# Down projection weights loaded as neighbouring rows, the activation written in even and odd order

## The reference

```
top_val, top_idx = lax.top_k(logits, TOP_K)            # 4 of 32
gates = jax.nn.softmax(top_val, axis=-1)
hgu = lax.ragged_dot(xs, w_gate_up, group_sizes) + b_gate_up[e_sorted]   # 1024 -> 2048
x_glu = jnp.minimum(hgu[..., ::2], 7.0)
x_lin = jnp.clip(hgu[..., 1::2], -7.0, 7.0)
act = x_glu * jax.nn.sigmoid(1.702 * x_glu) * (x_lin + 1.0)              # 1024 per token
out = lax.ragged_dot(act, w_down, group_sizes) + b_down[e_sorted]        # 1024 -> 1024
out = out * gates.reshape(-1)[order][:, None]
```

## Time and profile before

| | |
|---|---|
| three runs, median | 1988.65 us (1988.04 to 1990.12) |
| the profiled execution, its own time | 1986.01 us |
| its span, first to last instruction | 1984.3 us |
| mean granted clock of TensorE | 0.984 |
| TensorE / VectorE / ScalarE busy | 1932.5 / 1703.8 / 1372.4 us |
| one item of the loop, from one bias matmul to the same of the next item | 35.48 us |

### The profile page before, as it was taken

How to read it: one execution, slowest core, us unless ns; L and a number is a source line. 1 busy time by engine, 2 the same in 40 slices (tenths; PEclk the granted TensorE clock), 3 DMA queues, 4 the chain that set the end, 5 groups by cost and what they waited for, 6 DMA issues and landing times.

```text
span 1984.3 us, 29677 instructions
## 1 busy us (share of the span) xinstructions
PE 1932.5 (97%) x8812; PEld 1543.4 (78%) x8812; DVE 1703.8 (86%) x1759; ACT 1372.4 (69%) x1742; POOL 471.1 (24%) x339
## 2 busy tenths in 40 slices
PE   6999999998989999999999999999999999999998
PEld 3657767786768887888888888888888888888886
DVE  6899977349765479999999999999999999999998
ACT  4456855224345526888888888888888888888885
POOL 6671000000000108323222232222322223222231
PEclk7999999999999988999999999999999999999999
DMA  8222225332010256999999999999999999999995
GB/s 322 75 108 83 85 99 181 124 98 83 22 43 22 64 170 261 387 388 383 370 383 371 387 372 376 382 371 388 375 374 384 367 376 377 376 382 362 386 372 213
DMA packets 152207, 533.04 MB, mean 269 GB/s; under 512 B 14479, under 2 KB 19759, under 8 KB 149408
## 3 DMA queue, kind: packets, MB, share of 16 engines
q1 hardware_dynamic: 136112, 492.45, 65.6%
q0 software_dynamic: 16048, 39.99, 7.8%
HBM read 517.75 MB, written 24.26 MB: 273 GB/s over the span
## 4 chain that ended last, share of the span: by engine, by line
PE 89%; DVE 7%; DMA 1%; issue 1%; ACT 1%; SPq 0%; DVEq 0%; ACTq 0%
PE ps L979 55%; PE ps L1126 4%; PE ps L1174 4%; PE ps L917 3%; PE ps L1117 3%; PE ps L1155 2%; PE ps L1131 2%; PE ps L1350 2%; PE ps L1222 2%; PE ps L885 2%; PE ps L1016 2%; PE ps L856 1%; DMA arena<-in_w_down 1%; PE ps L1104 1%; PE ps L870 1%
## 5 line engine op out<-in xcount | busy, mean ns | idle before, releaser
L979 PE MATMUL ps<-split,xTs 128*128 128x512 f32 x3264 | 770.8, 392 | 0.7 <-ACT split L1798 0.5
L979 PEld LDWEIGHTS ps<-split,xTs 128*128 128x128 f32 x3264 | 610.9, 188 | 130.9 <-ACT split L1798 1.4
L2542 DVE TENSOR_TENSOR split<-arena,split 128x2048 fp32r<-128x2048 f32 x204 | 464.1, 2288 | 49.6 <-ACT split L1798 49.6
L1798 ACT ACTIVATE split<-arena 128x1024 fp32r<-128x1024 f32 x408 | 409.7, 1054 | 104.3 <-PE ps L979 103.6
L2542 DVE TENSOR_TENSOR split<-ring,split 128x2048 fp32r<-128x2048 f32 x204 | 466.0, 2317 | 0.1
L1798 ACT ACTIVATE split<-ring 128x1024 fp32r<-128x1024 f32 x408 | 410.8, 1056 | 66.6 <-PE ps L979 53.3
L979 PE MATMUL ps<-split,aTs 128*128 128x512 f32 x1632 | 386.0, 392 | 0.2 <-DVE split L2542 0.2
L979 PEld LDWEIGHTS ps<-split,aTs 128*128 128x128 f32 x1632 | 303.8, 188 | 63.2 <-DVE split L2542 0.6
L727 POOL DMA_INDIRECT arena<-h_rows,slots x33 | 91.7, 2780 | 338.5 <-PE ps L917 244.9
L775 POOL DMA_INDIRECT y_rows<-arena,slots x33 | 94.2, 2854 | 173.9 <-issue 102.3
L1960 DVE TENSOR_TENSOR split<-ring,split 128x2048 fp32r<-128x2048 f32 (+1 forms) x32 | 72.8, 2275 | 68.9 <-ACT split L1461 68.9
(11 more groups left out here) (435 smaller groups left out, 2539.3 us busy)
## 6 DMA issues: line engine op xcount, KB each, us to landing
ring<-in_w_gate_up SPq DMA_DIRECT2D x170, 1024.0 KB, 8.8
arena<-in_w_gate_up SPq DMA_DIRECT2D x102, 1024.0 KB, 7.4
arena<-in_w_down SPq DMA_DIRECT2D x102, 1024.0 KB, 10.4
ring<-in_w_down SPq DMA_DIRECT2D x34, 1024.0 KB, 10.8
ring<-in_w_in SPq DMA_DIRECT2D x23, 1024.0 KB, 5.0
ring<-in_w_out SPq DMA_DIRECT2D x8, 1024.0 KB, 5.2
ring<-in_mod_w SPq DMA_DIRECT2D x10, 512.0 KB, 9.1
ring<-in_mod_w SPq DMA_DIRECT2D x4, 1024.0 KB, 5.0
```

Of the source, the lines that this page charges most:

```text
L979: m = mm(ps[:, banks + q, :], lhs[:, x_, k, :], w[:, q * 512:(q + 1) * 512], start=start, stop=stop)
L1798: A(split[:, 0, c % SPLITS, :], chunk(c), ACT.Copy).then_inc(sig("hi_ready"), 1)
L2542: V.tensor_tensor(split[:, 1, s_, :].rearrange("p a b -> p (a b)"), chunk_pair(p), split[:, 0, s_, :].rearrange("p a b -> p (a b)"), ALU.s ...
```

## The change

The four `w_down` tiles are loaded so that partition p gets rows 2p and 2p + 1 of the tile's 256 rows, which are neighbours in HBM: one piece of 8 KB per partition in place of two of 4 KB. Chunk 0 of a tile then holds the even rows and chunk 1 the odd rows, and the activation has to be transposed in that order. To let the turns read neighbouring elements, VectorE writes each half of `actv` sorted: 256 even positions first, then the 256 odd ones. `clip_linear` still reads `ps` from left to right, so what it writes goes by turns to the two parts, 1 KB apart, and `activation` reads and writes `actv` in the same manner. `turn_pairs` takes the four blocks of 128 in the order 0, 2, 1, 3.

```
 def expert_tile(j, e):
     if j < 8:
         src = a["w_gate_up_2"][bass.ds(e, 1), g * 256:(g + 1) * 256, half * D:(half + 1) * D]
+        sp.dma_start(x.rearrange("p (k n) -> p k n", k=2), src.rearrange("o (k p) n -> p (o k) n", p=P)).then_inc(tile_ready[j % SLOTS], 16)
     else:
         src = a["w_down_2"][bass.ds(e, 1), (j - 8) * 256:(j - 7) * 256, :]
-    sp.dma_start(x.rearrange("p (k n) -> p k n", k=2), src.rearrange("o (k p) n -> p (o k) n", p=P)).then_inc(tile_ready[j % SLOTS], 16)
+        sp.dma_start(x, src.rearrange("o (p k) n -> p (o k n)", k=2)).then_inc(tile_ready[j % SLOTS], 16)
...
+def turn_pairs(x, bank):
+    for k in range(4):
+        c = k % 2 * 2 + k // 2
+        i = nc.tensor.transpose(ps[:, bank, k * P:(k + 1) * P], x[:, c * P:(c + 1) * P], IDENT)
+    return i
...
-turn(actv[:, 512:1024], 6).then_inc(sig("at_ps"), 1)
+turn_pairs(actv[:, 512:1024], 6).then_inc(sig("at_ps"), 1)
...
+def by_rows(half):
+    return actv[:, half * 512:(half + 1) * 512].rearrange("p (k m) -> p m k", k=2)

 def clip_linear(half):
-    V.tensor_scalar(actv[:, half * 512:(half + 1) * 512], gu[:, :, 1], LIMIT, -LIMIT, ALU.min, ALU.max)
+    V.tensor_scalar(by_rows(half), gu[:, :, 1].rearrange("p (m k) -> p m k", k=2), LIMIT, -LIMIT, ALU.min, ALU.max)

 def activation(half):
-    a_ = actv[:, half * 512:(half + 1) * 512]
+    a_ = by_rows(half)
-    V.scalar_tensor_tensor(a_, a_, 1.0, gsig[:, half, :], ALU.add, ALU.mult).then_inc(sig("act_ready"), 1)
+    V.scalar_tensor_tensor(a_, a_, 1.0, gsig[:, half, :].rearrange("p (m k) -> p m k", k=2), ALU.add, ALU.mult).then_inc(sig("act_ready"), 1)
```

More of the change, by code:

```diff
@@ L1019, in experts @@
                                 pe.wait_ge(sig("act_ready"), i * 2 + 1)
-                                turn(actv[:, 0:512], 6).then_inc(sig("at_ps"), 1)
+                                turn_pairs(actv[:, 0:512], 6).then_inc(sig("at_ps"), 1)
                             pair(4 * half + p, 2 * half, xTs, 2 * p, p == 0, p == 3)
```

## The result

The changed kernel takes 2000.19 us (median of 4 runs, 1997.06 to 2001.33); the kernel before, run beside it, took 1988.68 us (4 runs). The ratio worked out from the single runs is 1.0061, with a 95% interval of 1.0049 to 1.0072 (the two medians give 1.0058): slower by 0.6%, 11.5 us, where 2003 us had been forecast. The profiled execution took 1997.06 us, its span is 1995.4 us at a mean granted clock of 0.987.

A forecast was written before the change was run, and what follows sets the result against it. TensorE, busy 97% of the span, was taken to bound the kernel. 34 items x 0.42 = 14.3 us on the profiled 1986.0 gave 2000.3; with 2.6 us for the median, 2003 us, range 1987.5 to 2021.

The forecast's parts named there:

- TensorE bounds and has no wait; others have some reserve: In the loop: TensorE busy 97% of the span without long waits, VectorE next with 33.32 of 35.48 us per item.
- The transfer, the turns' order and SyncE cost and give nothing: Down tile loads in 8 KB pieces, reordered transposes and as many SyncE issues as before: 0 us each.
- Clip 0.33 and activation 0.41 us: Growth of VectorE's two instructions per half from 0.69 us, priced by a hopping read, plus a quarter for the activation's second hop.
- Half 0 late by 0.74, clip of half 1 by 0.11: VectorE 0.74 us late after half 0's activation; 0.63 us is absorbed before half 1's clip, leaving 0.11.
- End of the activation 0.69 us late: Half 1 on VectorE: 0.11 + 0.33 - 0.16 (cover by ScalarE's Sigmoid) + 0.41 = 0.69 us.
- The reserves: Lateness TensorE would not feel: 0.25 us (perhaps 0.48) at half 1's turns, 0.32 at next item's split 0, 0.85 at half 0's.
- 0.42 out of 0.37 to 0.44: TensorE's added wait per item, at half 1's turns and the next item's split 0: 0.37 to 0.44 us, 0.42 taken.
- rival B: Dear hops in clip and activation, read and write prices adding: 0.91 us per item, 31 us, 2020; chance 0.13 beyond 2017.
- A (free hops): Hops in clip and activation free or nearly so, all four instructions staying at 0.69 us: 1988.6 us; chance 0.16.
- C (faster matmuls): Larger transfer pieces end contention that slows TensorE's 48 down matmuls: 23 us gained, 1966; chance 0.03.
- D (slower landings): 8 KB pieces served 10% worse, so ScalarE waits for landings: at most 34 us more, 2023; chance 0.04.
- E: The transfer is cut into 4 KB pieces anyway: sum unchanged, costs nothing; called unlikely, no chance given.

## Why the prediction was right

The time was in the range, the direction was the one forecast, and 11.5 us were measured for the 14.3 of the sum. Step by step:

- *TensorE bounds and has no wait; others have some reserve.* Right, and the whole argument hangs on it: a growth of some 0.4 us in one instruction per half costs nothing (the clip) or 0.17 us per item (the activation), two cost 0.36, three cost 1.20.
- *The transfer, the turns' order and SyncE cost and give nothing.* Right. The kernel with hops alone has the ratio of the change, and the kernel with 8 KB loads and this order of the turns, but no hops, has that of before.
- *Clip 0.33 and activation 0.41 us.* The durations grew more, by 0.41 and 0.44 (1104 and 1133 ns). What is passed on to the next instruction is 0.34 and 0.37. The added quarter for the activation's second hop was wrong in kind: write alone and write with read cost the same within 8 ns. The 0.33 was the price of a read, taken for a write because no row had one; that it came near is luck. The 0.66 that the trace's 0.65 ns for a read was set beside is the table's figure for an output. For a source that hops the same table of the Trainium skill ("Vector Engine (DVE) Microarchitecture Reference", section 5.2) has 1.73 against 1.054, a difference of 0.68.
- *Half 0 late by 0.74, clip of half 1 by 0.11.* Split 8 started and ended 0.68 us late, and the clip started 0.05 late (0.97 us after pair 8 began, against 0.92).
- *End of the activation 0.69 us late.* 0.64 was measured (3.74 us after the start of pair 8, against 3.10): 0.05 + 0.17 at the gate part + 0.43.
- *The reserves.* This is the part that was off. At the turns I gave 0.25 with 0.48 as the other end. The other end is right for their start (0.64 late, first turn 0.17 late, 0.64 - 0.17 = 0.47), and another 0.06 us is lost by the loads without a lead. At split 0 I gave 0.32; it is 0.20. The 0.05 us between the end of what is waited for and the load held for the product too (0.04 and 0.06). What I left out is that the first product behind a late load takes 0.1 us more. But split 0 is only 0.56 us late and not 0.69, since it follows the activation's issue and not its end, and the clip was less late. 0.56 - 0.20 = 0.36, as measured. Both terms were 0.12 to 0.13 too large, and it is luck that they cancelled so exactly.
- *0.42 out of 0.37 to 0.44.* The lower end was the one with the right mechanism, all that split 0 waits. The upper one was the turns' wait with the reserve of 0.25, and the turns lost only 0.23 us. With 0.37 the sum would have been 12.6 us.
- *The sum of rival B* takes off 0.28 us, which is neither reserve. With the 0.32 of its own argument it is 0.87 us per item, 30 us and not 31. It changes nothing here.
- *Rivals.* A (free hops), C (faster matmuls) and D (slower landings) fell. For D: down tiles did land 0.3 us later, and the run with 8 KB loads and no hops takes the time of before. For C: 32 down matmuls take 7.56 us after the change and took 7.55. B fell as well, since both sides' prices fall together (the activation grew by 0.44, not by over 0.6). E fell by the packet counts.

## What to carry to other kernels

Before a neighbouring engine is given more work, read how long before it is needed each of its results is ready. In this loop what was under the smallest of these reserves (0.20 us) was free in one run, and what was above it was paid once per iteration in four. Take from the reserve what the wait itself costs: the matmul behind a late weight load took 0.1 us more. And moving the wait elsewhere doesn't help if it delays what the moved instructions release.

A write of 512 fp32 elements that goes by turns to two places 1 KB apart lasted 60% longer on VectorE. The same permutation was free in the reads of `ps`. A write in runs of two neighbours was free too, but it gives another order. A longer transfer piece gave nothing where nobody waited for landings.

## What the runs showed of the hardware

- A write of 512 fp32 elements that hops 1 KB at each one lasted 1104 ns instead of 688, 0.81 ns per element; the next instruction on VectorE started only 0.34 us later than before, 0.66 ns per element. The Trainium skill, "Vector Engine (DVE) Microarchitecture Reference", section 5.2, has 1.71 against 1.054 ns per column for a write that hops 4 KiB at each element, a difference of 0.66: it agrees with the distance between starts, not with the duration. It has 1.98 for three hopping streams; two of an activation's three streams hopped here and cost hardly more than the write alone (1133 and 1125 ns).
- Runs of two neighbours ended the price (688 ns), as that section says.
- Reads of `ps` at every fourth column cost what every second one does, on VectorE (687 and 686 ns) and ScalarE (678 ns).
- A weight load that reads every second column took 202 ns instead of 140, and a turn with it some 0.01 us more (0.08 us per item with eight of them).
- A weight load started 0.04 to 0.06 us after the end of what it waited for, on another engine: 1331.88 to 1331.92 behind a split, 1321.36 to 1321.42 behind the activation. The first matmul behind such a load took longer until the next one started. It was 0.33 us instead of 0.23 for a product of 512 columns (1331.94 to 1332.27). The first four turns took 0.49 us instead of the 0.44 of the run in which the clip alone hops.
